# Scores of two cache groups on VectorE instead of one, first sample buffers asked for earlier, and three weight loads moved to ScalarE's queue

## The reference

```python
DIL_GROUPS = ((128, 1), (512, 4), (2048, 16))
...
    kk = jnp.concatenate([buf[:, :, 0].astype(f32), k.astype(f32)], axis=1)
    vv = jnp.concatenate([buf[:, :, 1].astype(f32), v.astype(f32)], axis=1)
    idx = Lb + jnp.arange(T)[:, None] - dil * jnp.arange(span + 1)[None, :]
...
    s = jnp.einsum('bthd,btkhd->bthk', q.astype(f32), kg) * (D ** -0.5)
    s = jnp.where(valid, s, -jnp.inf)
    m = jnp.max(s, axis=-1, keepdims=True)
    p = jnp.exp(s - m)
    l = jnp.sum(p, axis=-1, keepdims=True)
    o = jnp.einsum('bthk,btkhd->bthd', p / l, vg)
```

## Time and profile before

| what | value |
|---|---|
| median of 3 runs | 2832.65 us |
| lowest and highest | 2830.3 and 2833.02 us |
| the profiled execution's own time | 2831.93 us |
| its span in the profile | 2830.1 us |
| PE busy | 2791.7 us (99%) |
| DVE busy | 1077.8 us (38%) |
| ACT busy | 865.1 us (31%) |
| POOL busy | 386.5 us (14%) |
| mean granted PE clock, share of full speed | 0.996 |
| bytes moved by DMA | 558.13 MB |

### The profile page before, as it was taken

The page is one execution under the profiler, slowest core; times in us unless marked ns, Lnnn a source line. Parts: engine busy times, 40 slices in busy tenths (PEclk is TensorE's granted clock), DMA queues, the critical chain, the costliest instruction groups (busy, mean ns, idle before and its releaser), DMA issues.

```text
span 2830.1 us, 40964 instructions
## 1 busy us (share of the span) xinstructions
PE 2791.7 (99%) x16232; PEld 1470.6 (52%) x16232; DVE 1077.8 (38%) x2399; ACT 865.1 (31%) x1770; POOL 386.5 (14%) x634
## 2 busy tenths in 40 slices
PE   8999999999999999999999999999999899999998
PEld 4444456565545665566555555555544344444444
DVE  6211134444333443444223323333324455555552
ACT  5101034444222222333223321111113444444441
POOL 2000000101311001130011113232300000000000
PEclk9999999999999999999999999999999999999999
DMA  9543454655577666584576759777736966556652
GB/s 282 130 167 130 161 186 150 212 173 189 186 257 278 202 186 192 197 257 160 185 263 218 257 157 329 249 252 248 240 139 188 313 173 175 144 153 179 162 111 57
DMA packets 320168, 558.13 MB, mean 197 GB/s; under 512 B 179117, under 2 KB 184053, under 8 KB 315993
## 3 DMA queue, kind: packets, MB, share of 16 engines
q1 hardware_dynamic: 268922, 296.71, 34.9%
q0 software_dynamic: 51056, 258.81, 27.4%
HBM read 378.84 MB, written 236.67 MB: 217 GB/s over the span
## 4 chain that ended last, share of the span: by engine, by line
PE 95%; DMA 2%; SPq 2%; DVE 1%; issue 0%; POOL 0%; ACT 0%; POOLq 0%; DVEq 0%
PE out L2592 42%; PE out L2182 22%; PE out L2589 15%; PE out L1119 2%; PE out L1104 2%; PE out L2595 2%; PE out L1110 1%; PE out L615 1%; PE out L626 1%; PE out L625 1%; PE out L1402 1%; PE out L1095 1%; PE out L1362 1%; PE out L590 1%; SPq L355 1%; DMA U<-stage 1%
## 5 line engine op out<-in xcount | busy, mean ns | idle before, releaser
L2592 PE MATMUL out<-w_hi,xn_hi 128*128 128x512 f16 x1920 | 729.2, 380 | 1.6 <-DMA xn_lo<-row0l 0.9
L2592 PE MATMUL out<-w_lo,xn_hi 128*128 128x512 f16 x1920 | 728.5, 379 | 0.0
L2592 PE MATMUL out<-w_hi,xn_lo 128*128 128x512 f16 x1920 | 728.4, 379 | 0.0
L2502 ACT ACTIVATE stage<-out 128x512 f32<-128x512 f32 (+1 forms) x170 | 99.4, 585 | 913.9 <-PE out L2592 604.4
L2536 DVE TENSOR_SCALAR stage<-out 128x512 f32<-128x512 f32 (+1 forms) x170 | 114.8, 675 | 650.2 <-PE out L2592 424.8
L2592 PEld LDWEIGHTS out<-w_hi,xn_lo 128*128 128x128 f16 x1920 | 188.1, 98 | 227.1 <-issue 1.1
L2592 PEld LDWEIGHTS out<-w_hi,xn_hi 128*128 128x128 f16 x1920 | 188.5, 98 | 208.1 <-issue 6.8
L2592 PEld LDWEIGHTS out<-w_lo,xn_hi 128*128 128x128 f16 x1920 | 188.2, 98 | 200.9 <-issue 0.8
L2589 PE MATMUL out<-xn_hi,w_hi 128*128 128x512 f16 x640 | 242.8, 379 | 0.0
L2589 PE MATMUL out<-xn_hi,w_lo 128*128 128x512 f16 x640 | 242.6, 379 | 0.0
L2589 PE MATMUL out<-xn_lo,w_hi 128*128 128x512 f16 x640 | 242.6, 379 | 0.0
(11 more groups left out here) (314 smaller groups left out, 4022.1 us busy)
## 6 DMA issues: line engine op xcount, KB each, us to landing
out<-in_cache_kv_w POOLq DMA_DIRECT2D x64, 1020.0 KB, 9.7
U<-stage SPq DMA_DIRECT2D x240, 256.0 KB, 4.8
raw<-in_w_in SPq DMA_DIRECT2D x78, 512.0 KB, 5.0
sw_kc<-in_cache_kv_w POOLq DMA_DIRECT2D x24, 1024.0 KB, 11.4
sw_vc<-in_cache_kv_w POOLq DMA_DIRECT2D x24, 1024.0 KB, 9.8
UT<-stage SPq DMA_DIRECT2D x80, 256.0 KB, 3.7
sw_rows<-U POOLq DMA_DIRECT2D x32, 512.0 KB, 7.5
out<-in_cache_kv_w POOLq DMA_DIRECT2D x16, 1008.0 KB, 7.7
```

What stands on the lines that cost most here:

```text
L2502: move_out(act, m, lambda o, x: act.activation(o, x, ACT.Copy, scale=1.0 / W_SCALE))
L2592: last = pe.matmul(out[m % 3][:, :], x[:, k, at:at + P], y[:, k, :], start=first, stop=final)
```

## The change

Four things change.

- `ROWED` goes from `(2,)` to `(1, 2)`: the four blocks of stride 4 are no longer transposed and multiplied by PE. DVE has eight steps per sample instead of four, one in each of the slots 1 to 8, with four row buffers. The flip moves from slot 8 to 9 and turns two tiles, the product with V from slot 12 to 13. The scores fit in one PSUM bank (408 columns instead of 792).
- The first loads of the samples stand at slot 515 instead of 522 and wait for the third head of the last window only; the memory of the buffers is laid out anew so that they overlap nothing that the fourth head uses. The fourth row buffer and the mask are asked for at slot 527, behind `windows.done`. DVE's clearing at slot 525 no longer waits for the windows' last store.
- The K pieces of the next sample are asked for in other slots (`FREED_SLOTS`).
- `queue_weights` goes from SP to ACT, at the same slot of the program and with the same wait.

```diff
--- before.py
+++ after.py
@@ -140,7 +140,7 @@
 N_CACHE = len(CACHE_BLOCKS)
 N_BLOCKS = N_CACHE + 1
 NEW_KEYS = GROUPS * DEC_SEQ
-ROWED = (2,)
+ROWED = (1, 2)
 TURNED_BLOCKS = [n for n, (g, _) in enumerate(CACHE_BLOCKS) if g not in ROWED] + [N_CACHE]
 N_TURNED = len(TURNED_BLOCKS)
 SCORES = TURNED_BLOCKS[:-1] + [("rows", g) for g in ROWED] + [N_CACHE]
@@ -979,12 +979,10 @@
     def __init__(self, bind, bank, U, UT, mask_in, identity, OG):
         sb, sem = bind
         self.U, self.UT, self.mask_in, self.identity, self.OG = U, UT, mask_in, identity, OG
-        self.qT = [sb(f"qT{s}", [P, SEQ]) for s in range(2)]
+        self.result, self.qT, self.k, self.v = zip(*[(sb(f"result{s}", [P, BLOCKS, HD + 2]), sb(f"qT{s}", [P, SEQ]), sb(f"k{s}", [P, BLOCKS, HD]),
+                                                      sb(f"v{s}", [P, BLOCKS, HD])) for s in range(2)])
         self.query = [sb(f"query{s}", [P, SPAN]) for s in range(2)]
-        self.k = [sb(f"k{s}", [P, BLOCKS, HD]) for s in range(2)]
-        self.v = [sb(f"v{s}", [P, BLOCKS, HD]) for s in range(2)]
         self.kT = sb("kT", [P, BLOCKS, P])
-        self.result = [sb(f"result{s}", [P, BLOCKS, HD + 2]) for s in range(2)]
         self.mask = sb("mask", [P, 2, P])
         self.score = [sb(f"score{s}", [P, 2, P]) for s in range(2)]
         self.prob = [sb(f"prob{s}", [P, 2, P]) for s in range(2)]
@@ -1075,10 +1073,19 @@
         return [(signal, n) for signal in (self.turned, self.turned_kept, self.scored, self.masked, self.top_ready, self.weighed,
                                            self.prob_turned, self.prob_kept, self.summed, self.result_kept)]
 
+    def head_done(self, eng, g, h):
+
+        eng.wait_ge(self.summed, (g * HEADS + h + 1) * BLOCKS)
+        eng.wait_ge(self.stored[h % 2], self.moved(g, h))
+
+    def read(self, eng):
+
+        eng.wait_ge(self.summed, GROUPS * self.STEPS)
+        eng.wait_ge(self.result_kept, GROUPS * self.STEPS)
+
     def done(self, eng):
-        wait(eng, self.summed, GROUPS * self.STEPS)
-        for h in range(HEADS - 2, HEADS):
-            wait(eng, self.stored[h % 2], self.moved(GROUPS - 1, h))
+        self.head_done(eng, GROUPS - 1, HEADS - 2)
+        self.head_done(eng, GROUPS - 1, HEADS - 1)
 
     def at(self, g, i):
 
@@ -1173,25 +1180,25 @@
     PAIR = 2
     CHUNKS = DEC_SEQ // PAIR
     STEPS = len(ROWED) * CHUNKS
-    EVERY = 2
-    RING = 3
+    EVERY = 1
+    RING = 4
     FIRST = 1
     FLIP_SLOT = FIRST + EVERY * (STEPS - 1) + 1
-    VALUE_SLOT = 12
-    FREED_SLOTS = {0: 3, 1: 4, 2: 6, 3: 10, 4: 5}
+    VALUE_SLOT = 13
+    FREED_SLOTS = {0: 3, 1: 6, 2: 8, 3: 10, 4: 3}
 
     def __init__(self, bind, bank, U, caches, mask_in, identity, OG):
         sb, sem, later = bind
         self.U, self.caches, self.mask_in, self.identity, self.OG = U, caches, mask_in, identity, OG
         self.kc = sb("sw_kc", [P, N_CACHE, WIDTH])
-        self.vc = sb("sw_vc", [P, N_CACHE, WIDTH])
         self.new_k = sb("sw_new_k", [P, WIDTH])
         self.new_v = sb("sw_new_v", [P, WIDTH])
         self.kn, self.vn = self.new_k[:NEW_KEYS, :], self.new_v[:NEW_KEYS, :]
         self.q_places = [(tile, QUAD) for tile in (self.new_k, self.new_v, sb("sw_q", [P, WIDTH]))]
+        self.rows = [sb(f"sw_rows{s}", [P, self.PAIR, WIDTH]) for s in range(self.RING)]
+        self.vc = sb("sw_vc", [P, N_CACHE, WIDTH])
         self.qT = sb("sw_qT", [P, GROUPS * HEADS, QUAD])
         self.kT = [sb(f"sw_kT{s}", [P, HEADS, P]) for s in range(2)]
-        self.rows = [sb(f"sw_rows{s}", [P, self.PAIR, WIDTH]) for s in range(self.RING)]
         self.sT = [sb(f"sw_sT{i}", [P, P]) for i in range(len(ROWED))]
         self.prob = sb("sw_prob", [P, KEYS])
         self.probT = sb("sw_probT", [P, N_BLOCKS, P])
@@ -1286,13 +1293,16 @@
 
     def queue(self, q, r):
         last = len(self.K_PIECES)
-        if r == -5:
+        if r == -12:
             self.load_q(q, 0)
             for p in range(last + 1):
                 self.load_k(q, 0, p)
                 if p == 0:
-                    for x in range(self.RING):
+                    for x in range(3):
                         self.load_rows(q, x)
+        if r == 0:
+            for x in range(3, self.RING):
+                self.load_rows(q, x)
             q.dma_start(self.mask[:, :], self.mask_in).then_inc(self.mask_loaded, 16)
         self.queue_rows(q, r)
         c, u = divmod(r, SAMPLE_PERIOD)
@@ -2337,9 +2347,11 @@
                     if g == 0:
                         sample_gla.done(q)
                 windows.queue(q, g, slot - WINDOW_SLOTS[g])
-            if slot == SAMPLE_SLOT - 5:
+            if slot == SAMPLE_SLOT - 12:
+                windows.head_done(q, GROUPS - 1, HEADS - 2)
+                cutter.done(q)
+            if slot == SAMPLE_SLOT:
                 windows.done(q)
-                cutter.done(q)
             samples.queue(q, slot - SAMPLE_SLOT)
 
         @block.sync
@@ -2366,10 +2378,6 @@
                 if p is not None:
                     load_raw(sp, PIECES * (n + 1) + p + RAW)
                 inputs.queue(sp, q)
-                if m == COLUMN_TILES * TOKEN_TILES - 1 and half == 1:
-                    for i in range(2):
-                        sp.wait_ge(out_ready[i], COLUMN_TILES * TOKEN_TILES // 2)
-                    mix.queue_weights(sp)
                 if half == 1:
                     sp.wait_ge(staged[e], j + 1)
                     if ROWS[t] == P and ORDER[n] in TURNED:
@@ -2500,6 +2508,10 @@
                         cut_hi_piece(act, PIECES * (n + 1) + p)
                     if half == 1 and m % 2 == 0:
                         move_out(act, m, lambda o, x: act.activation(o, x, ACT.Copy, scale=1.0 / W_SCALE))
+                    if half == 1 and m == COLUMN_TILES * TOKEN_TILES - 1:
+                        for i in range(2):
+                            act.wait_ge(out_ready[i], COLUMN_TILES * TOKEN_TILES // 2)
+                        mix.queue_weights(act)
                 inputs.scalar(act, q)
                 if q == LOWRANK_SLOT:
                     act.wait_ge(glr_loaded, 16)
@@ -2557,7 +2569,7 @@
                     windows.vector(dve, g, q - WINDOW_SLOTS[g])
                 sample_gla.vector(dve, q - GLA_SAMPLE_SLOT)
                 if q == SAMPLE_SLOT - 2:
-                    windows.done(dve)
+                    windows.read(dve)
                     samples.start(dve)
                 samples.vector(dve, q - SAMPLE_SLOT)
                 mix.vector_before(dve, q)
```

## The result

The changed kernel takes 2840.48 us in the median of 8 runs (2835.65 to 2846.58), the one before 2832.64 in as many beside it; the ratio is 1.0029, interval 1.0019 to 1.0038. **It is 8 us slower**, where 25 faster were forecast, and outside the range.

The account below looks back on a forecast made before the run. PE, busy 99% of the span, was taken to bound the kernel. First loads -10.4, side work -25.8, samples' stalls +18.1 and mixer weights -6.8 sum to -24.9 us, giving 2807 us, range 2795 to 2825.

Parts of the forecast that it names:

- First loads: Samples' first loads, asked for seven slots sooner: PE's wait for K blocks and the slow slot behind it go, -10.4 us.
- PE's side work: Transposes and products PE no longer does in the samples: 3.23 us a sample, eight times, -25.8 us.
- VectorE's pace: Flips of samples 1 to 7: DVE's own steps, move-outs and cuts stall PE, 10.6 us without sample 0.
- The ring of rows: Row loads for steps 4 to 7: 7 to 8 us available, landing 5.8 to 11.2, median 7.2; no stall added.
- so I take no more than what stands above: Row loads in samples: long landings stood behind a 1 MB K piece, so nothing added; 11.2 us kept for the range.
- The second rival: Rows late in every sample, landing 11.2 us: samples cost +40.5, sum -2.5, 2829 us; chance 0.12.
- Sample 0: First sample's flip: V asked for between row loads 4 and 5 delays rows; stall 6.5 us plus 2.2 of clock.
- I take 6.5, near the first: Sample 0's stall: 6.5 us chosen from 5 to 6.5, over 12.2 by the profile's row load behind V.
- The slow clock: PE at half speed after long waits: 2.2 us counted behind sample 0's stall, which exceeds 3.2 us.
- The mixer's weights: Last mixer weights moved from SP's queue to ACT's: wait falls from 7.0 to 3.1 us; term -6.8 us in all.
- and at the 426 of the stretch without transposes this takes 18.0 us: Mixer weights: 7.7 MB at 426 GB/s takes 18.0 us, to 2202.0, so PE waits 3.1 instead of 7.0.
- The weights gain nothing: Rival for the mixer: transfers share the same 16 DMA engines, so the term is near 0; 2814 us, chance 0.10.

## Why the prediction was wrong

The forecast was -24.9 us, the measured difference is +7.8. The flips of the samples with the clock behind them are 28 of the 33 us between the two, and the mixer's weights 9; the two parts that came right give back 3.

- **First loads: right.** -10.4 forecast, -11.0 alone.
- **PE's side work: right, a little small.** -25.8 forecast, -28.1 by the run that makes only four row loads.
- **VectorE's pace: right** to 0.3 us in every sample from 1 to 7.
- **The ring of rows: wrong, the step "so I take no more than what stands above".** It took the landing of 7.2 us from row loads that came one in two slots in the kernel before, and put it to loads that come one in a slot. Their median was 10.1, and those for the last four steps of sample 5 took 6.8, 8.5, 9.4 and 13.2. The second rival had this mechanism, with 11.2 in every sample; it got 0.12 because K pieces seemed to be the cause of long landings. Leaving them out took 1.3 us off the median landing and left the stalls at 36.2, so they aren't. With 256 different rows in place of the two that are spread, at the same rate, the landing was 6.4 and no stall of samples 1 to 7 was left above VectorE's pace. So the row loads delay each other, since each keeps the engines busy for longer than its bytes say. It cost 13.8 us. The landing of 11.2 that the second rival took for every sample came about in some only, most of all in sample 5.
- **Sample 0: wrong, the step "I take 6.5, near the first".** The profile had a row load behind the same V, at 16.5 us, and the text gave the stall for it, 12.2. It was 12.8. The reason for setting it aside, shift copies still queued, doesn't bear it out: in the kernel before they had landed by 1713.3, ahead of the row load asked for at 1715.81, and in the changed kernel by 1691, and its row load behind V still took 15.2. Asking for V later brought this stall to 2.3, so V was what stood in the way. It cost 6.3 us.
- **The slow clock: left out of the sum.** The earlier trace rows had it behind both long waits; the sum counted it in sample 0 only, and at 2.2, while it named a stall of 3.9 in sample 3 and none of clock. It cost 10.7 us, not 2.2. Stalls of 3.6 and 3.9 us lost more behind themselves (6.0 and 5.6 us at half speed) than those of 12.8 and 8.3 (3.3 and 3.2): the clock had fallen only 0.8 and 1.2 us before PE went on, and 10.2 and 3.6 us before in the long ones. The length of a stall alone doesn't give the price: the same 3.6 us in sample 3 lost 3.4 us at half speed in the run with four row loads.
- **The mixer's weights: wrong, the step "and at the 426 of the stretch without transposes this takes 18.0 us".** That priced the bytes of the weights and not the step beside them. The two m transposes were issued in 3.6 and 4.6 us ahead of the weights in one queue; with the weights on another queue they run at the same time, and the transposes take 9.7 and 12.2 and land after 24.5 and 15.7 (10.9 and 8.1 before). The load itself came as forecast, within 0.8 us, but PE's wait only changed its name: +1.8 instead of -6.8. Why the transposes take longer beside the weights is not settled. The Trainium skill (DMA: Bandwidth & Descriptors, "Issuing engines are not separate DMA queues") had this end, a term near 0. The trace agrees with it in the result; the rival that was made of it ("The weights gain nothing") held for this term, though its 2814 us did not, because of the other errors.

Together: -11.0 (A), -28.1 (B), +35.5 stalls (36.7 less 1.2), +10.7 clock behind them, +1.8 (D) is +8.9, against +7.8 measured. The 10.7 of the clock and the 10.7 of VectorE's pace are two different things that happen to have the same size; the pace is inside the 36.7.

## What to carry to other kernels

Here a landing time belonged to the rate at which loads were asked for (7.5 us in the median before, 10.1 at about twice the rate). When a change doubles the rate, price the load by the time it holds the engines (bytes moved and share of the stretch), and take for a load behind a backlog the row that stands behind that backlog. Moving a big load to another engine's queue freed nothing here; ask what stood ahead of it in the old queue and now runs beside it. Where one engine waits for another at a fixed point, a slot of room at that point may be worth more than the work removed: here one constant was worth 24 us, about as much as the whole change was forecast to gain.

## What the runs showed of the hardware

- Loads that spread the same two rows over 128 partitions kept the DMA engines busy 0.92 of the time at 275 GB/s, loads of different rows with the same bytes 0.78 at 278; the median landing was 10.1 against 6.4 us. Eight copies read 16 times each, in loads with about 127 more 4-byte packets, made it 0.98 and 11.1.
- The two m transposes on SyncE took 3.3 to 4.6 us to issue with the weights behind them in its queue (DMA share 1.12 at 242 GB/s in those 8 us of the kernel before, so the engines were not idle), and 8.0 to 12.2 beside 4 to 6 MB on ScalarE's queue. PE, which waits for their landing, lost what the sooner weights gave.
- Leaving out 3 MB of K or V in each of seven samples moved no stall by more than 1.7 us, though the DMA share fell from 0.92 to 0.79 and 0.74. The mean share of a stretch did not tell how late a single load was.
- Behind stalls of 2.9 to 12.8 us the clock was at half for 3.2 to 6.0 us of PE's work; in stalls of 8.3 and 12.8 us much of the half-speed stretch passed while PE stood and cost nothing.
